# A two-layer hybrid trunk on one core: mixer buffers laid over the expert-weight ring, a ring of 21 slots, ten experts of 64 slots

## What is computed

```python
for layer in range(DEPTH):                      # 2
    h = h + mixer[layer](rms_norm(h, norm_mix[layer]))
    u = rms_norm(h, norm_ffn[layer])            # (256, 1024)
    # router: best of 4 groups, then top 2 of its 8 experts -> comb (256, 32)
    for e in range(32):                         # hidden width 512
        act = silu(u @ w_gate[layer, e]) * (u @ w_up[layer, e])
        h = h + (act * comb[:, e:e+1]) @ w_down[layer, e]
return rms_norm(h, norm_final)
```

## Time and profile before

| | |
|---|---|
| median of the runs | 1544.51 us (1542.73, 1549.9, 1544.51) |
| the profiled execution, its own time | 1538.09 us |
| its span, first to last instruction | 1536.3 us |
| TensorE busy | 1403.4 us, 91% of the span |
| VectorE, ScalarE busy | 418.7 and 278.1 us |
| moved by DMA | 459.7 MB |
| expert chunks | 384 of 1024 KB |

### The profile page before, as it was taken

One profiled execution on the slowest core, in us unless ns is written; L12 is line 12 of the kernel. 1 busy time (PEld: TensorE's weight loads), 2 busy tenths in 40 slices (PEclk: granted clock), 3 DMA queues, 4 the chain that ended last, 5 costly groups with the idle time before them and its releaser, 6 DMA issues. The chain is left out here.

```text
span 1536.3 us, 22145 instructions
## 1 busy us (share of the span) xinstructions
PE 1403.4 (91%) x8946; PEld 780.2 (51%) x8946; DVE 418.7 (27%) x1025; ACT 278.1 (18%) x538; POOL 10.0 (1%) x12
## 2 busy tenths in 40 slices
PE   7999998899999999888699998988999999998884
PEld 3778884444444444333288886544444444443331
DVE  0148744311111121211135735223111111221112
ACT  2242322110101001000133553111010101000001
POOL 0000000000000000000000010000000000000000
PEclk9999979899999999999899998998999999999997
DMA  9410110999999999999463440149999999999992
GB/s 288 155 55 19 40 57 26 423 420 422 420 422 421 421 422 420 421 421 420 190 240 118 145 176 1 65 166 420 421 421 421 422 422 421 421 420 422 421 420 120
DMA packets 85453, 459.69 MB, mean 299 GB/s; under 512 B 10704, under 2 KB 16080, under 8 KB 36080
## 3 DMA queue, kind: packets, MB, share of 16 engines
q1 hardware_dynamic: 85360, 458.38, 73.8%
HBM read 457.30 MB, written 1.05 MB: 298 GB/s over the span
## 5 line engine op out<-in xcount | busy, mean ns | idle before, releaser
L1778 PE MATMUL bank<-rawffn,xgffn 128*64 128x512 f32 x1152 | 255.6, 596 | 0.0
L1722 DVE TENSOR_TENSOR aTffn<-bank,sgffn 128x256 f32<-128x256 f32 (+1 forms) x64 | 23.5, 367 | 638.4 <-ACT sgffn L1661 638.4
L1793 PE MATMUL bank<-rawffn,xgffn 128*32 128x512 f32 x896 | 147.5, 647 | 42.3 <-DMA rawffn<-in_moe_w_up 22.2
L1778 PEld LDWEIGHTS bank<-rawffn,xgffn 128*64 128x64 f32 x1152 | 81.4, 138 | 157.6 <-issue 155.7
L2342 PE MATMUL bank<-uT,wr 128*128 128x256 f32 x640 | 143.5, 384 | 0.0
L1747 PEld LDWEIGHTS bank<-selffn,uxffn 128*128 128x128 f32 x1024 | 125.8, 200 | 28.7 <-issue 26.8
L1816 PE MATMUL bank<-rawffn,aTffn 128*64 128x512 f32 x576 | 131.5, 598 | 9.1 <-DVE aTffn L1722 9.1
L1747 PE MATMUL bank<-selffn,uxffn 128*128 128x128 f32 (+1 forms) x1024 | 134.3, 287 | 3.3 <-DVE hitsffn L1554 2.0
L1658 ACT COPY gusffn<-bank 128x512 f32<-128x512 f32 x64 | 37.5, 585 | 532.3 <-PE bank L1778 316.9
L2342 PEld LDWEIGHTS bank<-uT,wr 128*128 128x128 f32 x640 | 121.7, 192 | 18.1 <-issue 1.9
L1840 PE MATMUL bank<-ysffn,selTffn 64*128 64x512 f32 x512 | 127.2, 615 | 1.7 <-DVE ysffn L1734 1.7
(11 more groups left out here) (360 smaller groups left out, 1237.4 us busy)
## 6 DMA issues: line engine op xcount, KB each, us to landing
rawffn<-in_moe_w_gate SPq DMA_DIRECT2D x128, 1024.0 KB, 24.4
rawffn<-in_moe_w_up SPq DMA_DIRECT2D x128, 1024.0 KB, 26.0
rawffn<-in_moe_w_down SPq DMA_DIRECT2D x128, 1024.0 KB, 25.7
wr<-in_ssm_w_in SPq DMA_DIRECT2D x10, 2048.0 KB, 8.7
wr<-in_hyb_w_in SPq DMA_DIRECT2D x5, 2048.0 KB, 8.0
wo<-in_ssm_w_out SPq DMA_DIRECT2D x4, 2048.0 KB, 10.9
gain<-in_rows SPq DMA_DIRECT2D x5, 512.0 KB, 12.9
wr<-in_hyb_w_in SPq DMA_DIRECT2D x1, 1760.0 KB, 14.1
```

Of the source, the lines that this page charges most:

```text
L1778: i = T.matmul(bank[GU_BANK][CAP * m:CAP * m + CAP, :], xg[:, odd, k, :], raw[:, slot, (k % 4) * FH:(k % 4 + 1) * FH], start=(k == 0), sto ...
L1793: i = T.matmul(bank[GU_BANK][CAP_S * c:CAP_S * c + CAP_S, :], xg_s[:, odd, 4 * half + k, :], raw[:, CHUNKS * ph + c, k * FH:(k + 1) * FH], ...
```

## The change

The ring gets 21 slots, so `FIXED`, the experts whose place doesn't depend on the router, is 4. Only the first 10 experts in order (4 fixed and 6 by count) have 64 slots, the other 22 have 32: 5 L pairs and 11 S pairs. Since an expert of the S pairs may now have over 32 tokens, the overflow test compares each count with its own cap, and the overflow block takes 20 experts at a time through a ring of two experts. The test moves behind the sort. The loops over pairs and over experts (SP's too) are written out in full; the waits on landed chunks become waits on constants for each slot.

All buffers of the mixers, the ring and the expert stage are placed by hand from one base (`Area`). A mixer's buffers are ordered by when they are last read, and SP issues chunks into the slots (8 KB each) that lie wholly below a mark as soon as the mark is reached:

| mixer | mark that SP waits for | chunks issued then |
|---|---|---|
| hyb | `out` 7 (the last attention output) | 0 to 5 |
| hyb | `qs` 1, 1 (end of `carried`) | 6 to 11 |
| hyb | `turnr` 1 (L991, second time) | 12 to 16 |
| ssm | `mgroup` 9 (end of `project(9, 1)`) | 0 to 4, then `wo2` of group 2 after `joined(0)` |
| ssm | behind it | 5 to 7 |
| ssm | `ssmy` 15, and `joined(1)` with `wo2` of group 3 | 8 to 11 |
| ssm | `gated` 3 | 12 and 13 |
| router, both layers | start of the block | up to 18, then the gain row |
| router, both layers | `uhi` 1 and `logits` (slots 19 and 20 hold `hg` and `uT`) | 19 and 20 |

```diff
-RING = 3
-FIXED = RING
-BIG = 18
-OVER = 12
+NSLOT = 21
+FIXED = -(-NSLOT // CHUNKS)
+BIG = 10
+OVER = FIXED + 16
+OVER_RING = 2
...
+    raw = ring_area("raw", [P, NSLOT, DC])
+    hg_, uT_ = (Area(AREA + (NSLOT - 2 + i) * SLOT_BYTES) for i in range(2))
...
+    def load_ahead(sp, layer, first, last):
+
+        for n in range(first, last):
+            load_chunk(sp, layer, n // CHUNKS, n % CHUNKS, n, raw_main[n])
...
+            sp.wait_ge(*at("out", 7))
+            load_ahead(sp, 0, 0, hyb_attended)
+            sp.wait_ge(*at("qs", 1, 1))
+            load_ahead(sp, 0, hyb_attended, hyb_carried)
+            sp.wait_ge(*at("turnr", 1))
+            load_ahead(sp, 0, hyb_carried, hyb_half)
...
         def router_sync(sp):
 
-            for e in range(FIXED):
-                for c in range(CHUNKS):
-                    load_chunk(sp, main_pass, e, e, c)
+            load_ahead(sp, layer, ahead[layer], NSLOT - 2)
             load_gain(sp, NORMS[2 * layer + 2])
+            sp.wait_ge(*at("uhi", tag, 1))
+            sp.wait_ge(*at("logits", tag))
+            load_ahead(sp, layer, NSLOT - 2, NSLOT)
...
-            sp.wait_ge(ps.s["order"], layer + 1)
-            with sp.Fori(1, EXPERTS // RING) as i:
-                for ph in range(RING):
-                    load_expert(sp, ps, b0, ordered_expert(sp, seq, i * RING + ph), i * RING + ph, ph, True)
-            for s in range(EXPERTS // RING * RING, EXPERTS):
-                load_expert(sp, ps, b0, ordered_expert(sp, seq, s), s, s % RING, True)
+            for n in range(NSLOT, NCHUNK):
+                s, c = divmod(n, CHUNKS)
+                if s < FIXED:
+                    e = s
+                elif c == 0:
+                    if s == FIXED:
+                        sp.wait_ge(ps.s["order"], layer + 1)
+                    e = ordered_expert(sp, seq, s)
+                was, piece = divmod(n - NSLOT, CHUNKS)
+                sp.wait_ge(ps.s["used"], USES * (b0 + was) + FREED[piece])
+                load_chunk(sp, layer, e, c, n % NSLOT, raw_main[n % NSLOT])
...
             def sort():
...
                     did(V.max(out=high[:, :], in_=now))
+                    if r == BIG // 8:
+                        did(V.tensor_scalar(caps[:, :], key[:, 0, :], high[:, BIG % 8:BIG % 8 + 1], float(CAP_S - CAP),
+                                            ALU.is_le, ALU.mult))
...
+                did(V.tensor_scalar(caps[:, :], caps[:, :], float(CAP), None, ALU.add))
+                did(V.tensor_tensor(count[:, :], count[:, :], caps[:, :], ALU.subtract))
+                did(V.tensor_reduce(over[:, 0:1], count[:, :], AX.X, ALU.max))
...
             for g in range(GROUPS):
+                if g == 2:
+                    sp.wait_ge(*at("mgroup", len(MG) - 1))
+                    load_ahead(sp, 1, 0, 5)
                 if g >= 2:
                     sp.wait_ge(*at("joined", g - 2))
                 load(sp, ("wj", "par")[g % 2], wo2[:, g % 2, :, :], wv_ssm[:, 4 * g:4 * g + 4, :])
+                if g == 2:
+                    load_ahead(sp, 1, 5, mam_projected)
+                    sp.wait_ge(*at("ssmy", MH // 2 - 1))
+            load_ahead(sp, 1, mam_projected, mam_scanned)
+            sp.wait_ge(*at("gated", GROUPS - 1))
+            load_ahead(sp, 1, mam_scanned, mam_gated)
```

More of the change, by code:

```diff
@@ new lines, in build @@
+    tiles_f, tiles_i = moe("tf", [P, 1]), moe("ti", [P, 1], I32)
+    key = moe("key", [P, EXPERTS // 8, EXPERTS])
+    count, caps = moe("count", [P, EXPERTS]), moe("caps", [P, EXPERTS])
+    over = moe("over", [P, 4])
+    high = moe("high", [P, 8])
+    ranked, seq = moe("ranked", [P, EXPERTS], U32), moe("seq", [P, EXPERTS], I32)
+    ss_, std_, rstd_ = (moe(n, [P, HALVES]) for n in ("ss", "std", "rstd"))
+    lgT = moe("lgT", [P, SEQ])
+    top, etop = (moe(n, [P, HALVES, 8]) for n in ("top", "etop"))
@@ new lines, in build @@
+    gus = moe("gus", [P, 4, P])
+    sg, aT = moe("sg", [P, 4, CAP]), moe("aT", [P, 4, CAP])
+    ys = moe("ys", [P, BANK])
+    NCHUNK = EXPERTS * CHUNKS
+    FREED = (1, 1, 2, 2, 3, 4)
+    raw_main = [sem(f"m_raw{c}") for c in range(NSLOT)]
+    raw_over = [[sem(f"o{layer}_raw{c}") for c in range(OVER_RING * CHUNKS)] for layer in range(2)]
+    moe_srcs = [[a[n][layer].rearrange("e (p k) f -> e p (k f)", p=P) for n in ("moe_w_gate", "moe_w_up", "moe_w_down")]
+                for layer in range(2)]
@@ new lines, in load_chunk, with main_piece @@
+    def load_chunk(sp, layer, e, c, slot, landed):
+        src, half = (moe_srcs[layer][c % 2], c // 2) if c < 4 else (moe_srcs[layer][2], c - 4)
+        sp.dma_start(raw[:, slot, :], src[bass.ds(e, 1), :, half * DC:(half + 1) * DC].rearrange(
+            "e p n -> p (e n)")).then_inc(landed, 16)
+    def load_ahead(sp, layer, first, last):
+        for n in range(first, last):
+            load_chunk(sp, layer, n // CHUNKS, n % CHUNKS, n, raw_main[n])
+    def main_piece(layer, s, c):
+        n = s * CHUNKS + c
+        slot = n % NSLOT
+        return slot, raw_main[slot], 16 * (layer * len(range(slot, NCHUNK, NSLOT)) + n // NSLOT + 1)
@@ L1649, in act_pass, with run @@
             evict_x(1, "gb", "xb", 0, False)
-            def run(t0, i):
-                small, next_small, first, last = pair_of(plan, t0)
-                t = i * len(LOOPED) + t0
+            def run(t):
+                small, next_small, first, last = pair_of(plan, t)
                 n, to = (CAP_S, sg_s) if small else (CAP, sg[:, :, :])
@@ L1734, in run, with pe_pass @@
                     V.tensor_copy(ys[:, :], bank[Y_BANK][:, :]).then_inc(S["y"], 1)
-            every_pair(dve, plan, looped, run)
-        def pe_pass(pe, ps, b0, p0, plan, looped, turns, opens):
+            for t in range(len(plan)):
+                run(t)
+        def pe_pass(pe, ps, b0, p0, plan, piece, opens):
             S = ps.s
@@ L1847, in pe_pass, with run @@
             gather_b(0, False)
-            def run(t0, i):
-                small, next_small, first, last = pair_of(plan, t0)
-                t = i * len(LOOPED) + t0
+            def run(t):
+                small, next_small, first, last = pair_of(plan, t)
                 pe.wait_ge(S["xa"], p0 + t + 1)
                 for odd in range(2):
-                    e, s0 = t * 2 + odd, 2 * t0 + odd
-                    ph = s0 % RING
-                    landed = ((turns(ph) + s0 // RING + 1) + i * (2 * len(LOOPED) // RING)) * 16
-                    (project_s if small else project)(odd, t, ph, landed)
+                    e = t * 2 + odd
+                    at_piece = lambda c: piece(2 * t + odd, c)
+                    (project_s if small else project)(odd, t, at_piece)
                     if not first or odd:
@@ L1868, in run @@
                     pe.wait_ge(S["act"], b0 + e + 1)
-                    (down_s if small else down)(ph, landed)
+                    (down_s if small else down)(at_piece)
                     if odd and not last:
                         gather_b(t + 1, next_small)
-            every_pair(pe, plan, looped, run)
+            for t in range(len(plan)):
+                run(t)
             pe.wait_ge(S["y"], b0 + 2 * len(plan))
@@ L2485, in _ @@
             joined(3)
-    mam.close()
+    ahead[1] = mam_gated
     experts(1)
```

315 lines of the change are left out of this document (149 added, 166 removed).

## The result

The median went from 1543.62 to 1496.48 us (four runs each; the changed kernel 1494.09 to 1501.27). The ratio is 0.9693, 95% interval 0.9655 to 0.9732: 41 to 53 us less, 47 in the middle. The forecast was 1494. The profiled execution of the changed kernel took 1494.09 us with a span of 1492.2, 44.1 less than before. One execution of the kernel before among those beside experiments 1 to 4 took 4846.41 us; it is left out of their ratios.

The account below looks back on a forecast made before the run. The train of 190 chunks a layer was taken to bound the expert stages. Gains of 25.5 and 24.4 us, 49.9 in sum, took the profiled 1538.09 to 1488.2; with 6.4 for the median, 1494, range 1481 to 1510.

Parts of the forecast that it names:

- What bounds the kernel: Expert stages: the train of 190 chunks decides their length, 479.9 and 480.3 us, and TensorE's work doesn't.
- hidden anyway: Rival at the stage's end: TensorE decides there, so an earlier train brings nothing, within 8 us of 1544.5; chance 0.02.
- The early loads: Mixers: first chunks issue at about 229.7 and 963.9 us; all 21 are there before any slot comes free.
- mixers beside transfers: Ends of hyb and ssm: chunks moving beside them cost 0, at worst a few us.
- the output weights: End of ssm: wo2 of group 3 lands at 1006.6 us, wanted at 1009.5, so hidden with 3 us to spare.
- The train after the first free slot: Expert stages: 169 chunks at 2.485 us, 420.0, plus 2.6 of latency and 5.0 lost in L pairs.
- moved addresses: Buffers placed elsewhere: no gain or cost taken for it.
- Ten for eighteen: Expert stages, ten L experts for eighteen: 36.6 us less TensorE work a layer, but worth only 4 us a layer.
- The ring of 21: Start of the expert stages: three more chunks are there, 7.5 us, already in the sum.
- The catch-up after nine S experts: S pairs: TensorE gains 4.07 us on the chunks with each expert, catches up after 9, and 13 a layer wait.
- thin queue: Rival in L pairs: few chunks under way, batches show latency, up to 5 us more a layer, 1500 to 1520; chance 0.14.
- The rival of the lower clock: Waiting S pairs: an S expert takes 20.8 us at the lower clock, costing 153 us, time 1647; chance 0.02.

Follow-up runs that it names:

- Experiment 1: The kernel before with ten experts of 64 slots for eighteen, its loop having one round; 1541.24 us, ratio 0.9984.
- experiment 2: The changed kernel with eighteen experts of 64 slots again for ten; 1502.54 us, ratio 0.9729.
- experiment 3: The changed kernel with no chunk issued before a mixer's block ends; 1543.55 us, ratio 1.0002.
- experiment 4: The changed kernel with six experts of 64 slots for ten, so three L pairs; 1491.63 us, ratio 0.9657.
- experiment 8: The changed kernel with early chunks in hyb only, those of ssm taken out; 1519.48 us, ratio 0.985.
- experiment 9: The changed kernel with a 256-byte base, the four fixed experts first as two S pairs, then one L pair, the rest small; 1483.55 us, ratio 0.961.
- experiment 5: The changed kernel with the base of all hand-placed buffers rounded up to a multiple of 256 bytes; 1491.54 us, ratio 0.9655.
- experiment 10: The kernel before with 128 bytes set ahead of the ring, so that it begins on a multiple of 256; 1532.19 us, ratio 0.9917.
- experiment 6: The kernel before with 32 bytes set ahead of the ring, which begins at 37024 instead of 36992; 1546.56 us, ratio 1.0014.
- Experiment 11: The kernel before with SyncE's loop over experts written out and nothing else; 1545.4 us, ratio 1.0012.
- experiment 7: The changed kernel with a ring of 18 slots for 21, hyb issuing sixteen chunks; 1513.45 us, ratio 0.9801.

## Why the prediction was right, and where its terms were off

*What bounds the kernel* held. Experiment 1 takes TensorE's work away and leaves the time; experiment 3 takes the early chunks away and gives the whole gain back. The rival "hidden anyway" is dead by these two. The highest slice in the earlier trace rows is 423, where I had written 424; nothing hangs on it.

*The early loads* came where they were forecast: 231.5 for 229.7, and in ssm 941.9, which is 963.9 less the 22 us by which layer 0 had already ended earlier. The stretch of ssm from `joined` on is unchanged, and so is hyb from its first mark on (1.85 us later at `carried`, and still 1.85 at the second `turnr`), so "mixers beside transfers" at 0 was right, and the output weights were hidden. Experiments 3 and 8 give 23 to 24 us for each layer.

*The train after the first free slot* was mis-sized. I had 427.6 us for it; it is 722.32 - 291.12 = 431.2 in layer 0 and 1459.26 - 1028.41 = 430.9 in layer 1, so 6.9 us more in all. The term 2.485 us for a chunk was taken from the kernel before and carried over; the steady pace is 419 GB/s for 421, which is 2 us in each layer. In layer 0 some 0.9 us of the rest lies at the change to S pairs, where the transfers fell to 341 GB/s for 5 us:

```profile
445.00:450.00 5.00, 4.75 (x39) 2.26 (x39) 1.46 (x5) 0.54 (x2) 0.00 (x0) 1.00 0.95 341
```

The first `project_s` begins at 440.96 and frees no slot before its end, as in experiment 9; that this makes the gap is argued and not tested. I had listed moved addresses as costing nothing. They aren't nothing: experiments 5 and 10 show that where the buffers lie moves the pace by over 1%. The 2.0 us for each transfer that I quoted from the Trainium skill (DMA: Bandwidth & Descriptors, Anatomy of one DMA) is given there for transfers that GpSimd issues, and these are SyncE's; the sum doesn't use it.

*The clock at the start* gave 4.6 us back that I hadn't counted, 2.3 in each layer. The first slot came free 26.0 us after the block's start in layer 1, 28.3 forecast, since the second gather and the first `project` ran at the higher clock (2.05 us for 3.79, and 7.09 us; 7.76 and 7.80 in the earlier trace rows). What the engine did before is the same in both kernels. It isn't the change's doing: in experiments 6 and 11, which are the kernel before with no edit to TensorE's code, the first `project` takes 7.09 us in both layers, and in the changed kernel's kin it takes 7.72 (experiment 2, layer 0), 7.78 and 7.80 (experiments 4 and 5, layer 1). What decides it stays open; each kernel was profiled once.

The rest is small: hyb ended 1.85 us later, after longer spells at 1.2 GHz well ahead of the first chunk (granted clock 0.91 for 1.00 from 100 to 120 us, first chunk at 231.47), and the stretches behind the last `project_s` are 1.6 us longer in all, with that of layer 1 at 6.59 us for 5.08. Hyb's end moves like this by itself: in experiment 6, where hyb is untouched, the expert stage begins its first matmul 8.3 us later than in the kernel before. Together: 1.85 + 6.9 - 4.6 + 1.6 = 5.8 us, which is 49.9 forecast less 44.1 measured.

So the mechanism was right, and the nearness of the number is in part luck. Without the 4.6 us of the clock the span's gain would be 10.4 us short of the forecast. The medians show more gain, 47 us, than the spans, since the profiled execution of the kernel before was a fast one, 1538.09 us with a median of 1543.62.

*Ten for eighteen* was put at 4 us a layer, 8 in both; experiment 2 has 6 in the medians and 4.3 in the trains behind the first freed slot. *The ring of 21* was put at 7.5 us a layer, 15 in both; experiment 7 has 17 us. *The catch-up after nine S experts* was right on the row, 538.71.

*The rival "thin queue"* was half there. In the L pairs the ring is full and few chunks are under way, 7 to 9 us from issue to landing for the 24.4 of the earlier trace rows (300 to 440 us). The pace is 407 to 411 GB/s, but that is TensorE's own 408, so no separate loss per transfer shows. *The rival of the lower clock* failed by its own test: in the windows 620 to 722 and 1320 to 1459 of the changed kernel TensorE has 0.97 of the clock:

```profile
620.00:722.00 102.00, 86.43 (x540) 35.97 (x535) 14.81 (x42) 8.28 (x20) 0.00 (x0) 0.97 1.01 419
1320.00:1459.00 139.00, 117.48 (x750) 49.56 (x746) 19.91 (x56) 11.13 (x27) 0.00 (x0) 0.97 1.01 419
```

TensorE waits for a chunk at most 1.5 us at a time there, and the clock is up nearly all the time; short spells at 1.2 GHz come even so, as in the 6.59 us of the last `project_s`. The Trainium skill's account of a kernel that falls back at each wait for a DMA (TensorE: Matmul & The Clock Gate, HAM oscillation) is of waits of 3 to 5 us, so it isn't the case of these. The trace shows that the rule which I drew from it, that every wait would throw the engine back, doesn't hold here: 0.97.

## What to carry to other kernels

When a stage streams weights at full rate, its length is the train from the first issue to the chunk the last matmul wants. Measure both paces for one piece, and then move the train's start, by giving its first buffers the memory that the stage before reads no more. Once the ring is full at the start, the next limits are the number of slots (2.5 to 2.8 us each here) and the moment at which the consumer gives the first one back: the small pair first cost 2.3 and 2.4 us there. Give the slots of such a ring an address that is a multiple of 256 bytes, and read the GB/s before and after. When two kernels differ by a few us, first lay their rows of unchanged code side by side: spells at 1.2 GHz in the mixers and routers moved single stages here by 2 to 8 us from one profiled kernel to the next.

## What was not expected of the hardware

The rate of the transfers into a ring of 8 KB rows moves with the ring's address in on-chip memory. A start on a multiple of 256 gave 426 to 427 GB/s (experiments 5 and 10), 128 or 160 over gave 421 (the kernel before, experiment 6), 32 over gave 419 (the changed kernel). In the kernel before this is worth 0.6 to 1.1% of the whole time. The other buffers moved too (all that are placed by hand in experiment 5, those behind the ring in experiment 10); that it is the ring's address is argued from this, that in these stretches the transfers go to the ring. The Trainium skill (DMA: Bandwidth & Descriptors, How a descriptor splits into AXI transactions) says that a transaction has to start on a multiple of 256 bytes. By that, an estimate, a row of 8 KB which doesn't start there needs one more, 33 instead of 32, or 3%. The direction agrees with the runs. The size doesn't: 427 for 421 GB/s is 1.4%, 426 for 419 is 1.7%, and the smallest offset is the slowest. Why 32 over is slower than 128 over stays open. Experiment 11 rules SP's code out, experiment 7 the number of slots (419 again with eighteen), experiment 3 the early chunks; the kernel before with a ring at 32 over a multiple of 256 was not tried.

The share of busy DMA engines doesn't tell a stream at its limit from one that waits for slots: it reads 1.00 at 407 GB/s and 1.01 at 427. The GB/s column tells them apart.
